# Block-wise neighbourhood attention for head pairs, and a mixture of experts in turns of three blocks with half blocks

## The reference, cut to what matters

```
c0 = clip(cidx - kw // 2, 0, GRID_W - kw)          # kw = 16, GRID_W = 64
in_win = (cidx[None, :] >= c0[:, None]) & (cidx[None, :] < c0[:, None] + kw)
s_nb = where(mask, s_nb + bias[None], NEG_INF)
p = softmax(concatenate([s_nb, s_cx], axis=-1), axis=-1)
```

```
xb = h[tok_b]
hid = silu(xb @ w_e_gate[e]) * (xb @ w_e_up[e])     # 1024 -> 256
return (hid @ w_e_down[e]) * w_b[:, None]           # 256 -> 1024
```

## Time and profile before

| | us |
|---|---|
| three runs: median, lowest, highest | 5358.55, 5353.62, 5374.47 |
| the profiled execution, its own time | 5338.49 |
| its span | 5336.6 |
| PE busy (share of the span) | 4601.7 (86%) |
| ACT, DVE, POOL busy | 904.6, 1373.5, 290.3 |
| experts' stage, from the first load (4301.7) to the first gather of Combine (5247.0) | 945.3 |
| neighbourhood attention, from 319.1 to 494.3 | 175.2 |
| granted TensorE clock, mean | 0.93 of 2.4 GHz |

### The profile page before, as it was taken

One profiled execution on the slowest core, in us unless ns is written; L12 is line 12 of the kernel. 1 busy time (PEld: TensorE's weight loads), 2 busy tenths in 40 slices (PEclk: granted clock), 3 DMA queues, 4 the chain that ended last, 5 costly groups with the idle time before them and its releaser, 6 DMA issues. The chain is left out here.

```text
span 5336.6 us, 37571 instructions
## 1 busy us (share of the span) xinstructions
PE 4601.7 (86%) x13404; PEld 2303.2 (43%) x13404; DVE 1373.5 (26%) x2472; ACT 904.6 (17%) x1691; POOL 290.3 (5%) x373
## 2 busy tenths in 40 slices
PE   6989799999789988979988886888889789988984
PEld 3445355555443433434434354333334444444442
DVE  1055333310311123043211245444410221111114
ACT  1023111100101011021101053233210111111110
POOL 0010100000100000000000031000000011111113
PEclk8989899999899998989999897888899899999996
DMA  5211311123131011212221060000112168888885
GB/s 222 95 39 55 114 51 51 50 77 137 63 119 41 32 37 43 76 51 75 73 69 52 31 256 32 16 24 20 36 59 71 52 240 320 318 311 312 310 317 215
DMA packets 138945, 608.52 MB, mean 114 GB/s; under 512 B 14464, under 2 KB 16512, under 8 KB 111952
## 3 DMA queue, kind: packets, MB, share of 16 engines
q1 hardware_dynamic: 103056, 472.02, 25.4%
q0 software_dynamic: 25696, 98.25, 5.1%
q10 hardware_dynamic: 10080, 36.70, 1.7%
HBM read 532.47 MB, written 74.45 MB: 114 GB/s over the span
## 5 line engine op out<-in xcount | busy, mean ns | idle before, releaser
L683 PE MATMUL ps<-arena 128*128 128x512 f32 (+1 forms) x2624 | 929.2, 517 | 26.4 <-POOLq L2379 23.0
L494 PE MATMUL ps<-arena 128*128 128x512 f32 (+1 forms) x1760 | 696.1, 557 | 36.7 <-DVEq L2379 22.5
L683 PEld LDWEIGHTS ps<-arena 128*128 128x128 f32 x2624 | 500.7, 191 | 456.4 <-issue 425.4
L2083 PE MATMUL ps<-arena 128*128 128x512 f32 x1120 | 522.7, 620 | 91.3 <-DMA arena<-w_gate_up 89.2
L584 PE MATMUL ps<-arena 128*128 128x512 f32 (+1 forms) x1472 | 487.3, 491 | 35.1 <-ACTq L2379 23.6
L494 PEld LDWEIGHTS ps<-arena 128*128 128x128 f32 x1760 | 335.3, 191 | 397.9 <-issue 349.3
L584 PEld LDWEIGHTS ps<-arena 128*128 128x128 f32 x1472 | 278.5, 191 | 250.7 <-issue 192.5
L2083 PEld LDWEIGHTS ps<-arena 128*128 128x128 f32 x1120 | 215.2, 197 | 355.9 <-issue 328.0
L634 PE MATMUL ps<-arena 128*128 128x512 f32 x768 | 338.0, 603 | 11.7 <-DVEq L2379 10.0
L1243 PE MATMUL ps<-arena 128*128 128x512 f32 x640 | 277.3, 595 | 9.1 <-POOLq L2379 6.8
L2095 PE MATMUL ps<-arena 128*128 128x512 f32 x560 | 252.0, 592 | 1.0 <-DVE arena L2190 1.0
(11 more groups left out here) (274 smaller groups left out, 3899.3 us busy)
## 6 DMA issues: line engine op xcount, KB each, us to landing
arena<-w_gate_up SPq DMA_DIRECT2D x140, 1024.0 KB
arena<-ada SPq DMA_DIRECT2D x144, 512.0 KB, 5.8
arena<-w_down SPq DMA_DIRECT2D x70, 1024.0 KB, 8.9
arena<-ffn_in SPq DMA_DIRECT2D x88, 512.0 KB, 3.6
y_rows<-arena ACTq DMA_DIRECT2D x70, 512.0 KB, 9.4
y_rows<-arena POOLq DMA_DIRECT2D x8, 4096.0 KB, 47.4
arena<-ffn_out SPq DMA_DIRECT2D x32, 512.0 KB, 3.6
arena<-ret_qk SPq DMA_DIRECT2D x16, 512.0 KB, 4.9
```

The lines of the kernel that those rows point to most:

```text
L494: mm = pe.matmul(k.ps[:, 2 * s + t % 2, 0:w], lhsT=k.ring[:, u % SLOTS, (c % 8) * P:(c % 8 + 1) * P], rhs=self.rhs[:, c, o:o + w], start=c ...
L683: mm = pe.matmul(k.ps[:, 2 * s + j % 2, 0:w], lhsT=k.ring[:, u % SLOTS, c * P:(c + 1) * P], rhs=k.H[:, c, o:o + w], start=c == 0, stop=c = ...
L2083: mm = pe.matmul(k.ps[:, p, :], lhsT=m.xT[:, p, c, :], rhs=m.WG[:, p, c, :], start=c == 0, stop=c == KD - 1)
```

## The change

1. **Latent tokens in blocks.** `ModLinear` may write its latent columns in the order of four column blocks, each of 8 rows by 16 columns (128 tokens), with a scale (0.125 for the queries); POOL copies `k.H` in this order (8 copies of 128x512), and `TokLinear` makes the values from that copy.
2. **Neighbourhood attention.** A step is now a pair of heads and a query block: 24 steps. A latent block needs the keys of its own column block and of the neighbours: 3 blocks (2 at the edges) instead of 4, plus the context. Scores of the two heads use partitions 0 to 63 and 64 to 127 of the array; probabilities of the second head are divided on POOL; transposes go through one PSUM bank in pieces of up to four; masks and bias are made by POOL, one tile of the pair's bias at a time.
3. **Experts in turns of three blocks.** A block with more than 64 rows is full, else half; `moved` turns as many half blocks into full ones as levels the two counts. A turn takes two full blocks and one mixed block, of which PSUM partitions 0 to 63 belong to one expert and 64 to 127 to another; its products are pairs of 64-column matmuls. The number of turns is the larger of both counts, halved and rounded up. There are four weight slots (two lie in the ring of weight units and in `k.H`) and three of every other buffer, so a load now waits for the block three before. Results of half blocks lie in `y_rows` from row 8192 on.
4. **Rows skipped.** Entries of the list that hold no token are out of bounds, and the gather leaves them out.
5. **Routing** has more DVE steps and one more PE product for this.

The core of the diff:

```diff
@@ class Neighbourhood, tensor @@
-            lhsT = self.QK[hp:hp + 64, h // 2, q * P:(q + 1) * P]
-            if q < LTT:
-                pe.matmul(k.ps[:, b, 0:T], lhsT=lhsT, rhs=self.QK[hp:hp + 64, 4 + h // 2, 0:T], start=True, stop=True)
...
+            part(0, T, N, w).then_inc(k.sig("context_scored").sem, 1)
+            part(0, lo * P, hi * P, 0)
+            part(1, lo * P, hi * P, L)
+            pe.wait_ge(k.sig("context_scored").sem, self.cx + LTT * hp + q + 1)
+            part(1, T, N, 0).then_inc(k.sig("scores_ready").sem, 1)
...
         scores(0)
-        for i in range(n + 2):
+        for i in range(n + 3):
+            if 2 <= i < n + 2:
+                turn(i - 2, 0)
+            if i >= 3:
+                out(i - 3, 0)
+            if 2 <= i < n + 2:
+                turn(i - 2, 1)
             if i + 1 < n:
                 scores(i + 1)
-            if i >= 2:
-                out(i - 2)
-            if 1 <= i <= n:
-                turn(i - 1)
+            if 2 <= i < n + 2:
+                turn(i - 2, 2)
+            if i >= 3:
+                out(i - 3, 1)
@@ class Neighbourhood, scalar @@
+        for i in range(n + 4):
+            if i >= 4:
+                out(i - 4)
+            if 2 <= i < n + 2:
+                turn(i - 2, 0)
+            if i < n:
+                exps(i)
+            if 2 <= i < n + 2:
+                turn(i - 2, 1)
+                turn(i - 2, 2)
@@ class Experts @@
+    BANK = (0, 1, 7)
+    PARTS = (((0, 0, P),), ((1, 0, P),), ((2, 0, P // 2), (3, P // 2, P)))
...
-            sp.wait_ge(k.sig("gate_up_made").sem, i * 2 + b - 1 + PRIME)
...
-            sp.wait_ge(k.sig("down_made").sem, i * 2 + b - 1 + PRIME)
...
+        with sp.Fori(0, self.turns(sp)) as i:
+            for slot, (j, at) in enumerate(((0, 0), (1, 1), (2, FULL), (2, FULL + 1))):
+                e = sp.value_load(m.expert[:, bass.ds(i * 2 + at, 1)], min_val=0, max_val=NE - 1)
+
+                sp.wait_ge(k.sig("gate_up_made").sem, i * 3 + j - 2 + PRIME)
+                for half in range(2):
+                    sp.dma_start(m.WG[slot][:, 4 * half:4 * half + 4, :],
...
+                sp.wait_ge(k.sig("down_made").sem, i * 3 + j - 2 + PRIME)
+                sp.dma_start(m.WD[slot], self.w_down[bass.ds(e, 1)].rearrange("a p c f -> p (a c) f"))\
...
+                                        bounds_check=T - 1, oob_is_err=False)\
...
             for c in range(KD):
-                mm = pe.matmul(k.ps[:, p, :], lhsT=m.xT[:, p, c, :], rhs=m.WG[:, p, c, :],
-                               start=c == 0, stop=c == KD - 1)
+                for slot, lo, hi in self.PARTS[j]:
+                    mm = pe.matmul(k.ps[lo:hi, self.BANK[j], :], lhsT=m.xT[:, j, c, lo:hi], rhs=m.WG[slot][:, c, :],
+                                   start=c == 0, stop=c == KD - 1)
```

More of the change, by code:

```diff
@@ new lines, in blocks, with width, tiles, keys @@
+    def blocks(q):
+        return (max(q - 1, 0), min(q + 2, LTT)) if q < LTT else (0, 0)
+    @classmethod
+    def width(cls, q):
+        lo, hi = cls.blocks(q)
+        return (hi - lo) * P
+    @classmethod
+    def tiles(cls, q):
+        return cls.width(q) // P + 2
+    def keys(self, q, e):
+        window, context = list(range(*self.blocks(q))), [LTT, LTT + 1]
+        return window + context if e == 0 else context + window
+    def scores_of(self, i, e):
+        q = self.its[i][1]
+        w = self.width(q)
+        o = (i % 2) * 3 * 512
+        lo = (512 - w, 768)[e] if w else (512, 1024)[e]
+        return self.k.ps.rearrange("p a b -> p (a b)")[:, o + lo:o + lo + w + L]
@@ L875, in scores @@
[L875 to L884, removed]
+                pe.wait_ge(k.sig("exp_ready").sem, self.e_rdy + i - 1)
@@ L952, in vector @@
-        n = len(self.its)
-        for i in range(n + 2):
-            if i < n:
-                scores(i)
-            if 1 <= i <= n:
-                turn(i - 1)
-            if i >= 2:
-                out(i - 2)
+            p = self.p[:, i % 3, 0, 0:self.tiles(q) * P]
+            dve.tensor_scalar(p, p, st[:, 4:5], None, ALU.mult).then_inc(k.sig("probs_ready").sem, 1)
+        for i in range(n + 1):
+            if i < n:
+                largest(i)
+            if i >= 1:
+                weigh(i - 1)
@@ L1923, in vector @@
         dve.wait_ge(k.dve.sem, k.dve.value())
[L1924 to L1930 removed]
+        dve.scalar_tensor_tensor(out=halves, in0=halves, scalar=float(FULL * P), in1=first, op0=ALU.add, op1=ALU.subtract)
@@ L2116, in tensor @@
-        turn_x(0, 0, 0)
-        pairs = pe.value_load(m.pairs, min_val=MINB // 2, max_val=MAXB // 2)
-        step(0, 0, 0, first=True)
-        with pe.Fori(0, pairs - 1) as i:
-            step(i, 1, 1)
-            step(i, 0, 2)
-        step(pairs - 1, 1, 1, last=True)
+                down(i, b)
+        turn_x(0, 0)
+        turns = self.turns(pe)
+        step(0, 0, first=True)
+        step(0, 1)
+        with pe.Fori(0, turns - 1) as i:
+            step(i, 2)
+            step(i, 3)
+            step(i, 4)
@@ new lines, in scalar @@
+        take_x(0, 0)
+        turns = self.turns(act)
+        silu(0, 0)
+        take_x(0, 1)
+        silu(0, 1)
+        take_x(0, 2)
+        take_y(0, 0)
+        with act.Fori(0, turns - 1) as i:
+            for b in (2, 3, 4):
+                silu(i, b)
+                take_x(i, b + 1)
+                take_y(i, b - 1)
+        silu(turns - 1, 2)
+        take_y(turns - 1, 1)
+        take_y(turns - 1, 2)
+        for j in range(3):
+            act.wait_ge(k.sig(f"y_stored{j}").sem, turns * 16 + 16)
+            act.copy(k.small[:, 31 + j:32 + j], m.w8[:, 0, 0:1])
```

624 lines of the change are left out of this document (365 added, 259 removed).

## The result

The changed kernel took 5029.14 us (median of 4 runs, 5019.03 to 5044.41), the kernel before 5356.09 (4 runs): ratio 0.9387, 95% interval 0.9352 to 0.9423. Predicted were 5076 us, in a range from 5010 to 5220. The profiled execution took 5034.65 us, of which 5032.6 are its span.

A forecast was written before the change was run, and what follows sets the result against it. Experts were taken as bound by transfers, with PE close and buffer depth partly limiting; attention by PE's many small instructions. 5338.5 - 229 (experts) - 58 (attention) + 5 (routing) = 5056.5, plus 20 for the median: 5076 us, range 5010 to 5220.

The forecast's parts named there:

- Turn of 38.5 us, 18 turns, -229: Experts: 18 turns of 38.5 us each make the stage 716 us against 945.3, so -229 us.
- The ends: Experts' stage: start and end outside the turns, taken as 13 + 2 + 8 = 23 us.
- PE's part, 35.0: Experts: PE's work per turn, two full blocks at 11.51 us and a mixed one at 12.0, 35.0 us.
- In line with the 36.9 of the transfers: Experts: PE's work plus one wait gives 36 to 38 us per turn; 15.1 MB at 409 GB/s take 36.9.
- 3% added for the clock: Experts: steady mean before lay 3% over clean blocks, clock 0.96 to 0.99; the same added, giving 38.5 us per turn.
- Attention -58: Neighbourhood attention: four pairs of heads at 25.6 us plus start and end, 117 us against 175.2, so -58 us.
- the 15 us: Attention: allowance for the stage's start and end, taken from before (175.2 - 160 = 15).
- Routing +5: Routing: some ten more small steps, one more PE trip and three more steps of 128x256, +5 us.
- +20 for the median: Whole kernel: median of the runs before lay 20 us above the profiled execution, so 20 us were added.
- The ceiling of 360 GB/s: Rival, experts' transfers: at 360 GB/s under mixed traffic a turn takes 42 us, the program 5139; chance 0.13.
- that rival: Rival, experts' mixed block: halves run one after the other, turn 46.1 us with 2%, program 5213; chance 0.10.
- the slower rival: Rival, experts: waits keep the clock at 1.2 GHz, PE has 70 us per turn, program 5640; chance 0.04.

The follow-up runs named there:

- the chain mended in two ways: Changed kernel with third and fourth slots' gate and up loads issued first, 5016.31 us; changed kernel with all weight loads in order of use, 5011.36 us.
- the last run: Changed kernel with weight loads in order of use and the padding rows gathered too: 5018.41 us.
- 4982: Changed kernel with weight loads in order of use and the fourth slot's down load left out: 4982.33 us.

## Why the prediction was right

The sign, the order of the terms and both mechanisms held; the time came out 47 us under the forecast, in my own range of 5017 to 5143.

- **Turn of 38.5 us, 18 turns, -229.** 37.92 us, 18 turns, -244.9. The ends cost 700.4 - 18 x 37.92 = 18 us, not 23. PE's part, 35.0, measured 34.8: the halves overlap, and the mixed forms cost 0.6 us per turn. One piece of the evidence for it was read too generously. DiffAttention's products last 130 us in sum for 50.0 us busy, a factor of 2.6; but full-width products overlap one another too, the 1120 of gate and up before with 620 ns each in 522.7 us busy, a factor of 1.33. Two halves side by side are the other factor of 2, as in the shared blocks (576 of 642 ns in 140.0 us).
- **"In line with the 36.9 of the transfers".** This sentence joined two things that the runs took apart. The wait (0.5 to 3.2 us, mean 2.3; I had said 1 to 3) comes, in this order of loads, from the chain that I described beside it: down load released late, gate and up load behind it, 3.15 MB in the time of one block. Taking bytes away behind the load in question did nothing, adding rows neither. The bytes are a second limit some 1 us per turn below: 36.8 and 36.4 us on the mean with the chain mended in two ways, 36.9 in the turns that wait. Only with both gone does PE's 34.8 appear.
- **3% added for the clock.** It was 0.7 us per turn, 2%, and in another place than I thought: not spread out, but in the first microseconds behind a wait.
- **Attention -58.** -68.4. The step that failed is "their weight loads follow one another, so I count no overlap": 20 output matmuls take 1.54 us and not 2.55, 352 of them 30.0 us busy and not 45. The stage came out 10 us under the forecast; a pair of heads takes 23.4 us (349.58 to 372.95), not 25.6. Against the 15 us stand terms that I had put too low: an edge step's scores take 1.45 us, not 1.05, and the ten transposes of an inner step 1.73, not 1.45. The 15 us do not pass into the time one for one in any case: 2 us more of output matmuls, in the run with the heads one after the other, did not show. POOL's reordering and the reordered copies cost nothing that shows: attention starts at 319.12 us before and after.
- **Routing +5.** From the token counts (before 4270.9, after 4205.8) to the first load it is 30.8 and 37.0 us, +6.3; 3.3 more us lie upstream, where nothing was changed; the run with the new attention alone, with the routing of before at the same 30.8 us, has 7.8 us more in this stretch (4243.9 - 429.5 = 3814.4), so they are spread between executions.
- **+20 for the median.** This step failed by its size alone: the profile of before lay 18 to 20 us under its median, that of the changed kernel 5 us above. One execution's distance from its median is no property of the next kernel. It makes 25 of the 47 us; the stages make the other 22.
- **Rivals.** The ceiling of 360 GB/s did not come: 400 to 404 in the page, 422 in a window of the last run. The Trainium skill's 358 GB/s for transfers between HBM and SBUF ("SBUF — State Buffer", Summary: rules for kernel authors) is exceeded in all of them, by one core alone on its chip. The halves overlapped, and only runs of 16 gave back most of what that rival priced (43.6 us per turn against 46.1). The clock did fall behind waits, but at the seams: at waits of 2 to 3 us a turn kept 0.98 to 0.99, at 12 to 15 us it fell to 0.84. The mechanism of the slower rival is real, and one block less of buffering brings it on, though in that run the lower clock makes 64 us of gate and up (281.2 + 166.6 busy against 256.3 + 127.6) and the waits 280. For the drain that "TensorEngine Tiling (Array Packing)", Key Properties, of the Trainium skill ascribes to a change of mode, the whole cost in the experts is at most those 0.6 us per turn.

The last version with the whole computation, loads in the order of use, takes 5011.36 us, 0.9372 of before, less than either kernel. The 29 us above 4982 go with 1.05 MB of weights per turn.

## What to carry to other kernels

Issue loads in the order in which the consumer frees their buffers: a load in a queue of waits starts when the slowest wait ahead of it ends, and bytes saved behind it then buy nothing. Here the order alone was worth 18 us of 5030. To learn whether bytes or the chain set a wait, take bytes away and add some, and do it again once the order is mended. A third buffer, with padding rows skipped and one block less, was worth more here (137 to 148 us of the experts' stage) than letting two small experts share a pass (108 us); and with one block less of depth the shared form lost 294 us of the stage.

## What I had not expected of the hardware

- Matmuls into the two column halves overlap without strict alternation: runs of 4 are nearly free (3.70 us against 3.65), runs of 6 save somewhat over half of what alternation does (1.15 us for 12 instructions, 0.88 alternating, 1.53 in one half), runs of 16 save some four instructions (12.28 us of 14.1).
- Behind a wait of 2.17 us the granted clock was 0.50 for 3 us, while behind one of 2.91 us the 32 matmuls took their full-speed 7.09 us. On the mean a wait of 2.3 us cost 0.7 us more than itself. What decides which waits are followed by it was not tried.
- The rate of the DMA engines at share 1.00 to 1.02 was 403, 411, 418 and 422 GB/s in four kernels that differ only in the order of loads and the rows gathered.
